# Storing query and key tiles as high and low parts already in the projection of a one-core hybrid attention block

## The chip, the cores and the metric

The kernel runs on one core of one Trainium2 chip. The time is the device time of one launch in microseconds (us). Before the change three runs took 1384.02, 1390.10 and 1389.47 us, median 1389.47. The execution that the profiler recorded took 1383.56 us.

## The reference

One decoder block on x of 1024 tokens by 1024 channels, in float32. All weights are float32 and are read once.

```
h    = modulate(rms_norm(x), sh1, sc1)              # adaLN from c
proj = h @ w_in                                     # q_d k_d v_d | iq ik iw | q_f k_f v_f | f_logit
DSA (8 heads of 64): score = sum_h iw_h relu(iq_h . ik);  keep the 256 best keys of each query
                     softmax over the kept keys, rope on the first 16 channels of q_d, k_d
FoX (8 heads of 64): softmax(q k / 8 + cum_q - cum_k), causal, cum = cumsum(log_sigmoid(f_logit + b))
x    = x + g1 * (rms_norm(o_d) | rms_norm(o_f)) @ w_out
h    = modulate(rms_norm(x), sh2, sc2);  x = x + g2 * (silu(h @ w_gate) * (h @ w_up)) @ w_down
out  = rms_norm(x)
```

## The kernel before

It is one program without loops at run time. Every engine has its list of instructions, and semaphores alone tie the lists together. Engines are named as in the profile: PE multiplies matrices, DVE (VectorE), ACT (ScalarE) and POOL (GpSimd) work on elements, SP issues all DMAs, in its own order.

A float32 product is computed as three products of fp32r operands: each operand is split into a high part (a rounding copy) and a low part (value less high). Who does the splitting, and when, is what the change is about.

**Projection.** `w_in` is taken in seven chunks (`CHUNK_COL`): chunk 0 holds what the selection and the gates need, chunks 1 to 6 hold FoX q, k, v and DSA q, k, v, in this order. A chunk of 512 columns has eight tiles of 24 matmuls (`tile`, `three`). The tiles go round four PSUM banks, so PE may start tile n once tile n-4 has been copied out (`pj_ev`). ACT copies each tile out (`evac_tile`) to one of two halves of `stage`, and SP stores it to DRAM: q and k to `qk_scratch`, laid out with channels as rows, v to `v_scratch`. POOL splits the four weight pieces of the next chunk (`split`: one CAST and one TENSOR_TENSOR of 128x1024 for each).

**Selection.** Beside the projection DVE finds for each query the 256th best score by bisection: 32 steps (`bisect`), each of four counts on DVE and two on ACT (`sign_counts`) and three to five tiny operations on 128x6 elements that form the next candidate. `PROJ_ORDER` deals the steps out over ACT's list: one or two steps between the copies of two tiles. Then `choose` turns the scores of query tiles 2 to 7 into masks, eight operations for each tile. The first `CHOICE_EARLY` operations (four tiles) come before attention, the rest are dealt out one by one over attention's units (`CHOICE_TILES`).

**Attention.** 16 heads (0 to 7 FoX, 8 to 15 DSA) of eight units, one for each query tile of 128. For unit u PE forms the logits (`logits`), DVE adds the bias and finds the minimum (`biased`), ACT takes the exponential (`expo`), PE transposes (`turn`), ACT copies out, and PE multiplies with the values of a pair of heads (`values`). Logits run two units ahead. For a head's logits PE needs the high and low parts of q and k: `load_qk` loads q and k of the head, each twice over 64 partitions, to `Qd` and `Kd`, and POOL makes the parts (`prepare`: three CASTs and two TENSOR_TENSORs, two CASTs for a DSA head). `Qd` and `Kd` exist once, so `load_qk(hd + 2)` waits until `prepare(hd + 1)` is done. The rotation of DSA's q and k (`rotate`) is done by POOL in three parts, in heads 3 to 5.

In the same stretch DVE sums the adaLN rows (`modulation`, 32 operations on 128x1024, each on a 512 KB piece of `ada_w`), at the units that `MOD_TILES` names, and POOL splits `w_out` (`split_out`) in heads 12 to 14. The last half of projection tiles 6 and 7 of chunk 6 is done in head 0 (`HELD_AT`).

**After attention** come the output projection and a feed-forward part with Strassen-like sums. The change leaves both as they are.

## Time and profile before

| | |
|---|---|
| time of the profiled execution | 1383.56 us |
| its span | 1381.8 us |
| median of three runs | 1389.47 us (1384.02 to 1390.10) |
| PE busy | 1309.9 us, 95% |
| DVE busy | 1004.5 us, 73% |
| POOL busy | 851.4 us, 62% |
| ACT busy | 695.7 us, 50% |
| granted TensorE clock, mean | 0.986 of full speed |

The profile gives for each engine the time in which it worked. Matmuls are pipelined and overlap in the listing, so a busy PE may still be slower than it could be. The share of an engine is a mean over stages that have different limits, so the stages are looked at apart: the bisection beside the projection lies at 193 to 331 us, the rest of the projection to 364 us, attention at 364 to 613 us. 1.76 us of the time lie outside the span.

### The profile page before, as it was taken

The page shows a single profiled execution, that of the slowest core. Times are in us where ns is not written, and L with a number is a line of the kernel's source. Part 1 is how long each engine was busy: PE and PEld are TensorE (multiplying, and loading weights), DVE is VectorE, ACT ScalarE, POOL GpSimd, SP SyncE. Part 2 cuts the span into 40 slices and gives each one's busy share as a digit, 9 for nine tenths or more (in the row PEclk, how much of TensorE's full clock was granted, in tenths as well). Part 3 has the DMA queues.
Part 4 walks back from the last instruction along what each step waited for, and adds up shares of the span by engine and source line. Part 5 has one row for each costly group of instructions (what it writes and reads, how often), then busy time and mean ns, then how long its engine had stood idle before and what let it go on. Part 6 is the DMA issues. An engine that isn't in the chain of part 4 may idle for free.

```text
span 1381.8 us, 19486 instructions
## 1 busy us (share of the span) xinstructions
PE 1309.9 (95%) x6595; PEld 1069.4 (77%) x6595; DVE 1004.5 (73%) x1585; ACT 695.7 (50%) x1395; POOL 851.4 (62%) x552
## 2 busy tenths in 40 slices
PE   1999999999989999999999899999999999999996
PEld 0988778888767677678887688888888888788885
DVE  4563769999786888876569776655556667479998
ACT  6623345564478777774336344333444333554545
POOL 0261403324359744951027889988889984798995
PEclk9799999999999999999999999999999999999998
DMA  9131312342345776715100333233333234998873
GB/s 382 55 98 55 97 49 92 107 124 78 100 124 168 232 218 192 215 48 198 42 36 31 105 107 123 85 115 100 115 114 109 90 122 153 390 355 300 287 255 140
DMA packets 130379, 200.53 MB, mean 145 GB/s; under 512 B 10637, under 2 KB 65093, under 8 KB 129258
## 3 DMA queue, kind: packets, MB, share of 16 engines
q1 hardware_dynamic: 130282, 199.30, 43.2%
q8 instruction: 53, 0.87, 0.3%
q14 instruction: 44, 0.36, 0.1%
HBM read 156.99 MB, written 42.27 MB: 144 GB/s over the span
## 4 chain that ended last, share of the span: by engine, by line
PE 77%; DVE 10%; issue 4%; ACT 3%; DMA 2%; POOL 2%; SPq 1%; DVEq 0%; ACTq 0%; POOLq 0%
PE PS L2176 20%; PE PS L2177 20%; PE PS L2178 20%; PE PS L2393 4%; PE PS L2345 4%; DVE AS L2042 2%; PE PS L2364 2%; DMA ada<-in_ada_w_dram 1%; DVE BS L2047 1%; POOL WSf L1025 1%; PE PS L2369 1%; PE PS L2366 1%; DVE LP L1815 1%; POOL WS L1037 1%; DVE PS L2099 1%
## 5 line engine op out<-in xcount | busy, mean ns | idle before, releaser
L1037 POOL TENSOR_TENSOR WS<-WSf,WS 128x512 fp32r<-128x512 f32 x109 | 161.7, 1491 | 9.1 <-ACT WS L1347 9.1
L1347 ACT CAST WS<-WSf 128x512 fp32r<-128x512 f32 x110 | 68.5, 623 | 195.3 <-POOL WSf L1025 194.5
L1025 POOL TENSOR_TENSOR WSf<-rawg 128x512 f32<-128x512 f32 x55 | 77.7, 1412 | 115.5 <-PE PS L2178 110.8
L2176 PE MATMUL PS<-yh,WS 128*128 128x512 f32 (+2 forms) x360 | 139.2, 387 | 1.5 <-DVE yl L1956 1.5
L2177 PE MATMUL PS<-yl,WS 128*128 128x512 f32 (+2 forms) x360 | 138.9, 386 | 0.0
L2178 PE MATMUL PS<-yh,WS 128*128 128x512 f32 (+2 forms) x360 | 138.8, 385 | 0.0
L2176 PE MATMUL PS<-BS,AS 128*128 128x512 f32 x308 | 121.0, 393 | 3.9 <-DVE BS L2047 3.1
L2177 PE MATMUL PS<-BS,AS 128*128 128x512 f32 x308 | 120.4, 391 | 0.0
L2178 PE MATMUL PS<-BS,AS 128*128 128x512 f32 x308 | 120.3, 391 | 0.0
L1268 ACT ACTIVATE LP<-LP,nmin 128x128 f32<-128x128 f32 (+7 forms) x128 | 100.2, 783 | 36.5 <-DVE nmin L1815 35.1
L2042 DVE TENSOR_TENSOR AS<-rawa,AS 128x512 fp32r<-128x512 f32 x77 | 100.1, 1316 | 23.5 <-ACT AS L1406 23.3
L2176 PE MATMUL PS<-XH,WS 128*128 128x512 f32 x264 | 103.6, 392 | 6.2 <-POOL WS L1037 6.2
L1056 POOL TENSOR_TENSOR BS<-rawb,BS 128x512 fp32r<-128x512 f32 x57 | 90.4, 1591 | 27.9 <-ACT BS L1410 27.7
L2178 PE MATMUL PS<-XH,WS 128*128 128x512 f32 x264 | 103.3, 391 | 0.0
L2177 PE MATMUL PS<-XL,WS 128*128 128x512 f32 x264 | 103.2, 391 | 0.0
L1657 DVE TENSOR_SCALAR_CACHE_REDUCE marks_c<-sel,bis 128x640 f32<-128x640 f32 (+4 forms) x134 | 102.5, 819 | 0.6
L2345 PE MATMUL PS<-ident,LP 128*128 128x128 f32 x576 | 89.1, 279 | 8.1 <-ACT PTb L1258 3.7
L1049 POOL TENSOR_TENSOR rawb<-rawb 128x512 f32<-128x512 f32 x55 | 90.1, 1648 | 7.5 <-DMA rawb<-in_w_down_dram 7.5
L1170 ACT ACTIVATE PS<-sel,bis 128x896 f32<-128x896 f32 x64 | 67.6, 1057 | 49.9 <-DVE bis L1712 35.1
L2345 PEld LDWEIGHTS PS<-ident,LP 128*128 128x128 f32 x576 | 64.9, 141 | 30.5 <-ACT PTb L1258 9.7
L1025 POOL TENSOR_TENSOR WSf<-rawu 128x512 f32<-128x512 f32 x55 | 84.6, 1538 | 3.0 <-PE PS L2178 2.5
L1406 ACT CAST AS<-rawa 128x512 fp32r<-128x512 f32 x77 | 47.9, 622 | 76.0 <-PE PS L2178 64.8
(340 smaller groups left out, 3836.0 us busy)
## 6 DMA issues: line engine op xcount, KB each, us to landing
rawb<-in_w_down_dram SPq DMA_DIRECT2D x132, 256.0 KB, 4.8
rawa<-gu_scratch SPq DMA_DIRECT2D x77, 256.0 KB, 4.8
gu_scratch<-GS SPq DMA_DIRECT2D x55, 256.0 KB, 4.8
raw<-in_w_in_dram SPq DMA_DIRECT2D x24, 512.0 KB, 3.9
rawg<-in_w_gate_dram SPq DMA_DIRECT2D x22, 512.0 KB, 4.5
rawu<-in_w_up_dram SPq DMA_DIRECT2D x22, 512.0 KB, 4.4
ada<-in_ada_w_dram SPq DMA_DIRECT2D x8, 1024.0 KB, 15.1
qk_scratch<-stage SPq DMA_DIRECT2D x32, 256.0 KB, 2.2
```

The lines of the kernel that those rows point to most:

```text
L1025: pool.tensor_tensor(WSf[m % N_SLOT][:], left(i, mat, a), left(i, mat, b), ALU.add if sign > 0 else ALU.subtract).then_inc(ws_sum, 1)
L1037: pool.tensor_tensor(lo, WSf[m % N_SLOT][:] if b else left(i, mat, a), hi.bitcast(F32), ALU.subtract).then_inc(ws_ready, 1)
L1049: pool.tensor_tensor(r[:, 0, :], r[:, 0, :], r[:, 1, :], ALU.add if RIGHT[DOWN[m // PAIRS]][2] > 0 else ALU.subtract).then_inc(gb_sum, 1)
L1056: pool.tensor_tensor(b[:, 1, :], rawb[m % DOWN_RAW_B][:, 0, :], b[:, 0, :].bitcast(F32), ALU.subtract).then_inc(gb_lo, 1)
L1268: act.activation(LP[:, u % 3, 0:n], LP[:, u % 3, 0:n], ACT.Exp, bias=nmin[:, u:u + 1], scale=-1.0, accum_out=sums[:, u:u + 1]).then_inc(ex ...
L1347: act.copy(WS[m % N_SLOT][:, 0], src).then_inc(ws_hi, 1)
L1657: did(dve.tensor_scalar(marks[0][:, n_tk % 2, 0:P * (t + 1)], view(t), limit, 0.0, op, ALU.add, accum_out=col(0, t)))
L2042: dve.tensor_tensor(AS[m % DOWN_SLOTS][:, 1, :], rawa[m % DOWN_RAW_A][:], AS[m % DOWN_SLOTS][:, 0, :].bitcast(F32), ALU.subtract).then_inc ...
L2176: pe.matmul(dst, left[0], right[0], start=first, stop=False)
L2177: pe.matmul(dst, left[0], right[1], start=False, stop=False)
L2178: return pe.matmul(dst, left[1], right[0], start=False, stop=last)
L2345: last = pe.transpose(dst[:, i * P:(i + 1) * P], src, ident[:])
```

## The change

- The chunks are taken in the order 0, FoX v, FoX q, FoX k, DSA q, DSA k, DSA v. `TURNED`, the chunks of q and k, becomes 2, 3, 4, 5 in place of 1, 2, 4, 5.
- For a tile of q or k ACT copies out twice, once to `stage` as float32 and once to `stage_h` as fp32r, the high part. POOL subtracts the two to `stage_l` (`low_tile`). SP waits for the subtraction and stores high and low part, two DMAs of 256 KB for one before.
- `load_qk` loads the parts from DRAM to where PE reads them, six DMAs of 256 KB for four before, and waits until PE has read the logits of head hd - 2 (`qk_pe`). `Qd`, `Kd` and `prepare` are gone. Head 1 gets a place of its own.
- The rotation adds high and low, rotates and splits again, twelve operations of 128x1024 in one run on POOL for six in three runs. Its loads and stores double.
- Three query tiles are chosen before attention for four before, and 24 operations of `choose` for 16 lie inside it, in heads 0 to 4.
- No modulation lies in head 4, and four lie in head 5.
- `split_out` is no longer tied to heads: POOL does it when the data is there.

```diff
-CHUNK_COL = [COL_IDX, COL_FOX, COL_FOX + GW, COL_FOX + 2 * GW, 0, GW, 2 * GW]
+CHUNK_COL = [COL_IDX, COL_FOX + 2 * GW, COL_FOX, COL_FOX + GW, 0, GW, 2 * GW]
-CHOICE_TILES = ((2, 4, 6, 7), (1, 2, 3, 5, 6, 7), (1, 2, 3, 5, 6, 7))
+CHOICE_TILES = ((2, 4, 6, 7), (1, 3, 5, 6, 7), (1, 2, 3, 5, 6, 7), (1, 3, 5, 6, 7), (1, 2, 3, 4))
-MOD_TILES = {hd: (6, 7) if hd < 6 else (1, 2, 6, 7) for hd in (*range(4, 12), 13)}
+MOD_TILES = {hd: (1, 2, 6, 7) for hd in (*range(5, 12), 13)}
-CHOICE_EARLY = 4 * CHOICE_OPS
+CHOICE_EARLY = 3 * CHOICE_OPS
-TURNED = (1, 2, 4, 5)
-VALUES = (3, 6)
+TURNED = (2, 3, 4, 5)
+VALUES = (1, 6)
+LOW_AHEAD = ((0, 1), (2,), (3,), (4,))
...
             def load_qk(hd):
                 b, first, row = hd % 2, 0 if hd < NH else 2, hd % NH * DH
-                if hd >= 1:
-                    sp.wait_ge(k_lo, hd)
-                    sp.wait_ge(q_lo, hd)
-                for i, dst in enumerate((Qd, Kd)):
-                    for half in range(2):
-                        sp.dma_start(dst[half * DH:(half + 1) * DH, :],
-                                     qk_dram[first + i, row:row + DH, :]).then_inc(qk_in[b], 16)
+                i = qk_home(hd)
+                if hd >= 2:
+                    sp.wait_ge(qk_pe, TT * (hd - 1))
+                q_high, q_low, k_high, k_low = (dram[first + e, row:row + DH, :] for e in range(2) for dram in (qk_dram, qk_low_dram))
+                sp.dma_start(QT[i][0:DH, :].bitcast(F32), q_high).then_inc(qk_in[b], 16)
+                sp.dma_start(KA[i][0:DH, :].bitcast(F32), k_high).then_inc(qk_in[b], 16)
+                sp.dma_start(QT[i][DH:P, :].bitcast(F32), q_low).then_inc(qk_in[b], 16)
+                sp.dma_start(KA[i][DH:P, :].bitcast(F32), k_high).then_inc(qk_in[b], 16)
+                if hd < NH:
+                    sp.dma_start(CQ[0:DH, b, :].bitcast(F32), q_high).then_inc(qk_in[b], 16)
+                    sp.dma_start(CK[0:DH, b, :].bitcast(F32), k_low).then_inc(qk_in[b], 16)
...
                     sp.wait_ge(pj_ev, TT * ch + t + 1)
                     if ch in TURNED:
+                        sp.wait_ge(pj_lo, TT * (ch - TURNED[0]) + t + 1)
...
-                if hd == 1:
+                if hd == 3:
                     sp.wait_ge(qk_pe, TT)
+                    sp.wait_ge(tp_ev, group_no["C", 3] + 1)
                     for i in range(2):
-                        sp.dma_start(RX[i][:], rope_rows(i)).then_inc(rx_in, 16)
+                        sp.dma_start(RX[i][:], rope_rows(qk_dram, i)).then_inc(rx_in, 16)
+                        sp.dma_start(RT[i][:], rope_rows(qk_low_dram, i)).then_inc(rx_in, 16)
...
-                if hd >= 1:
-                    load_qk(hd + 2)
+                load_qk(hd + 2)
...
+            def low_tile(ch, t):
+                n = TT * (ch - 1) + t
+                pool.wait_ge(pj_ev, TT * ch + t + 1)
+                pool.tensor_tensor(stage_l[:, n % 2, :], stage[:, n % 2, :], stage_h[:, n % 2, :].bitcast(F32),
+                                   ALU.subtract).then_inc(pj_lo, 1)
...
-            def prepare(hd):
-                b, i = hd % 2, 0 if hd == 0 else 2 - hd % 2
-                pool.wait_ge(qk_in[b], 64 * (hd // 2 + 1))
-                if hd >= 2:
-                    pool.wait_ge(qk_pe, TT * (hd - 1))
...
                 if n >= 2:
-                    act.wait_ge(stage_out[n % 2], 16 * (n // 2))
-                act.mul(stage[:, n % 2, :], PS[:, q % 4, :], -SOFT if ch in (1, 4) else 1.0).then_inc(pj_ev, 1)
+                    act.wait_ge(stage_out[n % 2], stores_ahead(n))
+                last = act.mul(stage[:, n % 2, :], PS[:, q % 4, :], QK_SCALE.get(ch, 1.0))
+                if ch in TURNED:
+                    last = act.mul(stage_h[:, n % 2, :], PS[:, q % 4, :], QK_SCALE[ch])
+                last.then_inc(pj_ev, 1)
...
                 if t == 0:
-                    pe.wait_ge(k_lo, hd + 1)
-                    pe.wait_ge(q_lo, hd + 1)
+                    pe.wait_ge(qk_in[hd % 2], 96 * (hd // 2 + 1))
```

The first place is POOL's list in the projection, where the weight pieces of the next chunk are split. `wl`, `wh` are weights, `raw` the loaded piece. Before:

```order
L898 CAST wl<-raw 128x1024
L900 TENSOR_TENSOR wl<-raw,wl 128x1024
L898 CAST wl<-raw 128x1024
L900 TENSOR_TENSOR wl<-raw,wl 128x1024
L898 CAST wh<-raw 128x1024
L900 TENSOR_TENSOR wh<-raw,wh 128x1024
```

Now, at the same splits:

```order
L924 CAST wl<-raw 128x1024
L926 TENSOR_TENSOR wl<-raw,wl 128x1024
L932 TENSOR_TENSOR stagel<-stage,stageh 128x512
L924 CAST wl<-raw 128x1024
L926 TENSOR_TENSOR wl<-raw,wl 128x1024
L932 TENSOR_TENSOR stagel<-stage,stageh 128x512 x5
L924 CAST wh<-raw 128x1024
L926 TENSOR_TENSOR wh<-raw,wh 128x1024
```

Every tile of a q or k chunk brings one subtraction (L932) between the splits. Three of the five in a row belong to the end of one chunk, two to the start of the next.

The second place is SP's list at the first pieces of `ada_w` for the modulations (`adar`), with what the DMA waits for. Before, in the pass for head 3:

```order
L672 DMA Qd<-qk_scratch 64x1024 [waits q_lo,k_lo]
L672 DMA Qd<-qk_scratch 64x1024
L672 DMA Kd<-qk_scratch 64x1024 x2
L663 DMA Vn<-v_scratch 128x4x128 [waits pv_pe]
L663 DMA Vn<-v_scratch 128x4x128
L776 DMA g1b<-in_ada_b_dram 1x1024 [waits md_ms]
L776 DMA mod<-in_ada_b_dram 1x1024 x2
L725 DMA adar<-in_ada_w_dram 128x1024 [waits tk_done]
```

Now, in the pass for head 4:

```order
L685 DMA QT<-qk_scratch 64x1024 [waits qk_pe]
L686 DMA KA<-qk_scratch 64x1024
L687 DMA QT<-qk_low_scratch 64x1024
L688 DMA KA<-qk_scratch 64x1024
L690 DMA CQ<-qk_scratch 64x1024
L691 DMA CK<-qk_low_scratch 64x1024
L749 DMA adar<-in_ada_w_dram 128x1024 [waits tk_done]
L749 DMA adar<-in_ada_w_dram 128x1024
```

The first modulation stood at unit 6 of head 4 and stands at unit 1 of head 5. Its piece now comes behind the six loads of head 6, and these wait until PE has done the last logits of head 4.

## Rows read from the trace of the kernel before

**Rows 1.** DVE in time, around the bisection: start us, us, line, operation

```profile
193.41 0.17 DVE L1692 TENSOR_TENSOR bis<-bis 128x6 f32<-128x6 f32 x1
...
207.21 2.29 DVE L1692 TENSOR_TENSOR bis<-bis 128x6 f32<-128x6 f32 x1
...
233.86 0.61 DVE L1657 TENSOR_SCALAR_CACHE_REDUCE marks_c<-sel,bis 128x384 f32<-128x384 f32 x1
...
236.92 0.17 DVE L1692 TENSOR_TENSOR bis<-bis 128x6 f32<-128x6 f32 x1
...
237.32 0.17 DVE L1712 TENSOR_TENSOR bis<-bis 128x6 f32<-128x6 f32 x1
...
237.52 0.61 DVE L1657 TENSOR_SCALAR_CACHE_REDUCE marks_c<-sel,bis 128x384 f32<-128x384 f32 x1
...
330.23 0.17 DVE L1692 TENSOR_TENSOR bis<-bis 128x6 f32<-128x6 f32 x1
```

**Rows 2.** POOL in time, one weight split of the projection

```profile
207.09 2.39 POOL L900 TENSOR_TENSOR wh<-raw,wh 128x1024 fp32r<-128x1024 f32 x1
```

**Rows 3.** POOL's 128x512 subtraction elsewhere: ns shortest/median/longest, first and last start

```profile
L1037 POOL TENSOR_TENSOR WS<-WSf,WS x109: 1263/1304/2246, 717.7 to 1140.2; 128x512 fp32r<-128x512 f32 x109
```

**Rows 4.** ACT in time, copies of projection tiles: [idle before <-releaser]

```profile
236.04 0.58 ACT L1145 ACTIVATE stage<-PS 128x512 f32<-128x512 f32 x1
...
328.81 1.06 ACT L1145 ACTIVATE stage<-PS 128x512 f32<-128x512 f32 x2
...
336.69 0.60 ACT L1145 ACTIVATE stage<-PS 128x512 f32<-128x512 f32 x1 [4.56 <-PE PS L2178]
```

**Rows 5.** DVE in time, the last tile chosen before attention and the first bias

```profile
353.78 0.61 DVE L1741 TENSOR_SCALAR sel<-sel,bis 128x768 f32<-128x768 f32 x1
...
360.10 0.56 DVE L1764 TENSOR_SCALAR sel<-sel 128x768 f32<-128x768 f32 x1
364.21 0.29 DVE L1815 CUSTOM_DVE_ANT_0 LP<-PS,strip 128x128 f32<-128x128 f32 x1 [3.55 <-PE PS L2366]
```

**Rows 6.** Stretches, attention by pairs of heads: us, busy by engine, clock, DMA share, GB/s

```profile
193.00:331.00 138.00, 138.00 (x610) 114.28 (x609) 131.47 (x370) 82.43 (x149) 46.32 (x29) 1.00 0.32 101
...
364.00:393.30 29.30, 26.15 (x161) 20.20 (x160) 24.56 (x45) 21.70 (x54) 21.46 (x12) 1.00 0.52 140
393.30:425.90 32.60, 29.92 (x221) 22.47 (x222) 23.11 (x44) 24.75 (x63) 21.30 (x12) 1.00 0.30 71
...
456.20:485.00 28.80, 26.54 (x191) 19.47 (x189) 25.23 (x45) 23.00 (x59) 20.78 (x10) 1.00 0.79 255
485.00:514.70 29.70, 29.52 (x224) 22.95 (x224) 23.49 (x42) 23.05 (x61) 15.09 (x9) 1.00 0.72 231
514.70:545.50 30.80, 28.75 (x213) 21.20 (x209) 26.70 (x48) 24.43 (x61) 16.08 (x9) 1.00 0.63 189
545.50:582.00 36.50, 34.59 (x241) 25.88 (x243) 29.09 (x58) 28.00 (x67) 26.98 (x14) 0.95 0.68 202
582.00:613.00 31.00, 29.39 (x204) 20.88 (x205) 28.84 (x61) 24.56 (x62) 19.95 (x11) 1.00 0.34 103
```

**Rows 7.** SP, POOL and PE in time, from the load of head 8 to its logits

```profile
470.06 1.12 SPq L672 DMA_DIRECT2D Qd<-qk_scratch  x2
...
477.15 1.04 POOL L935 CAST QT<-Qd 128x1024 fp32r<-128x1024 f32 x1 [7.17 <-DMA Kd<-qk_scratch]
...
481.73 3.23 POOL L943 TENSOR_TENSOR QT<-Qd,QT 64x1024 fp32r<-64x1024 f32 x1
...
485.04 1.09 SPq L672 DMA_DIRECT2D Qd<-qk_scratch  x2
...
485.07 0.30 PE L2364 MATMUL PS<-KA,QT 128*128 128x128 f32 x1 [0.88 <-issue]
```

**Rows 8.** DVE's modulations of one kind: ns shortest/median/longest

```profile
L1830 DVE SCALAR_TENSOR_TENSOR mod<-adax,cact,mod x14: 1274/1280/3368, 473.2 to 580.8; 128x1024 f32<-128x1024 f32 x14
```

**Rows 9.** DVE in time, a choice and a modulation beside busy POOL

```profile
405.58 3.36 DVE L1756 SCALAR_TENSOR_TENSOR marks_d<-marks_d,bis 128x1024 f32<-128x1024 f32 x1
...
580.82 3.37 DVE L1830 SCALAR_TENSOR_TENSOR mod<-adax,cact,mod 128x1024 f32<-128x1024 f32 x1
```

More of the change, by code:

```diff
@@ L203, with stores_through, stores_ahead @@
     GB_TARGET.append((GB_TARGET[_m - DOWN_RAW_B] if _m >= DOWN_RAW_B else GB_BASE[_m]) + (32 if _m in DOWN_SUMS else 16))
-GU_BASE = dict(zip(DOWN, 2 * [8 * (NC - 1) * TT] + [16 * MOD_SLOT.count(0), 16 * MOD_SLOT.count(1)] + 2 * [64 * V_PARTS] + [16]))
+GU_BASE = dict(zip(DOWN, 2 * [8 * TT * (NC - 1 + len(TURNED))] + [16 * MOD_SLOT.count(0), 16 * MOD_SLOT.count(1)] + 2 * [64 * V_PARTS] + [16]))
+def stores_through(ch):
+    return 8 * TT * sum(2 if c in TURNED else 1 for c in range(1, ch + 1))
+def stores_ahead(n):
+    return sum(32 if 1 + m // TT in TURNED else 16 for m in range(n % 2, n, 2))
 def done_first(t):
@@ L355, in build @@
         g1b = at(32, "g1b", [P, D])
-        QT = [at(kb, f"QT{i}", [P, SEQ], F32R) for i, kb in enumerate((180, 40, 52))]
-        KA = [at(kb, f"KA{i}", [P, SEQ], F32R) for i, kb in enumerate((184, 44, 56))]
+        QT = [at(kb, f"QT{i}", [P, SEQ], F32R) for i, kb in enumerate((180, 40, 52, 172))]
+        KA = [at(kb, f"KA{i}", [P, SEQ], F32R) for i, kb in enumerate((184, 44, 56, 176))]
         KB = [at(kb, f"KB{i}", [P, SEQ], F32R) for i, kb in enumerate((188, 48, 60))]
@@ L686, in _ @@
             for ch in range(1, NC):
-                if ch == 5:
-                    for i in range(2):
-                        sp.wait_ge(stage_out[i], 16 * 3 * TT // 2)
-                    sp.wait_ge(sc_pe, IH * (TT - FIRST_TOPK))
-                    load_qk(0)
                 if ch == 6:
@@ L696, in _ @@
                     load_cum(1)
+                    for i in range(2):
+                        sp.wait_ge(stage_out[i], stores_through(3))
+                    sp.wait_ge(sc_pe, IH * (TT - FIRST_TOPK))
+                    load_qk(0)
                 for t in range(TT):
@@ L700, in _ @@
                     if ch in TURNED:
+                        sp.wait_ge(pj_lo, TT * (ch - TURNED[0]) + t + 1)
+                    if ch in TURNED:
                         f, half = divmod(t, 2)
-                        dst = qk_dram[QK_BASE[ch], f * P:(f + 1) * P, half * BANK:(half + 1) * BANK]
-                    else:
-                        dst = v_dram[VALUES.index(ch), t * P:(t + 1) * P, :]
-                    sp.dma_start(dst, stage[:, q % 2, :]).then_inc(stage_out[q % 2], 16)
+                        for dram, held in ((qk_dram, stage_h), (qk_low_dram, stage_l)):
+                            sp.dma_start(dram[QK_BASE[ch], f * P:(f + 1) * P, half * BANK:(half + 1) * BANK],
+                                         held[:, q % 2, :].bitcast(F32)).then_inc(stage_out[q % 2], 16)
+                    else:
+                        sp.dma_start(v_dram[VALUES.index(ch), t * P:(t + 1) * P, :], stage[:, q % 2, :]
+                                     ).then_inc(stage_out[q % 2], 16)
                     if t < PIECES and ch + 1 < NC:
                         load_piece(PIECES * (ch + 1) + t)
-                    if ch == 6 and t == 4:
+                    if ch == 6 and t == 2:
+                        for i in range(2):
+                            sp.wait_ge(stage_out[i], stores_through(5))
                         load_qk(1)
-                    if ch == 6 and t == TT - 2:
-                        load_qk(2)
                 if ch == 4:
@@ L904, in _ @@
                 w = IDXW if ch == 0 else GW
+                if ch - 1 in TURNED:
+                    for t in LOW_AHEAD[n % PIECES]:
+                        low_tile(ch - 1, t)
                 if ch == 0:
@@ L916, in _ @@
                 split(n, hi[:, 0:2 * w], lo[:, 0:2 * w], held, rounded=ch == 0).then_inc(w_ready, 1)
+                if ch - 1 in TURNED and n % PIECES == PIECES - 1:
+                    for t in range(LOW_AHEAD[-1][-1] + 1, TT):
+                        low_tile(ch - 1, t)
             pool.wait_ge(pj_pe, (NC - 1) * TT)
             pool.wait_ge(w_ready, N_PROJ)
+            pool.wait_ge(pj_lo, TT * len(TURNED))
             pool.memset(CQ[DH:DH + 4].bitcast(F32), 1.0).then_inc(strip_ok, 1)
@@ L986, in _ @@
                 pool.tensor_copy(spread[i][:], angle[:].unsqueeze(2).to_broadcast([P, TT, REPS, HALF])).then_inc(spread_ok, 1)
-            for hd in range(2 * NH):
-                if 1 <= hd and hd + 1 < 2 * NH:
-                    prepare(hd + 1)
-                    if hd + 1 in ROPE_HEADS:
-                        rotate(ROPE_HEADS.index(hd + 1))
-                    if hd == 3:
-                        for dst in (g1b, mod23):
-                            pool.memset(dst[:], 0.0).then_inc(md_ms, 1)
-                    if hd == 9:
-                        pool.wait_ge(tp_ev, group_no["M", 5] + 1)
-                        pool.memset(mod23[:, 0, :], 0.0).then_inc(md_ms, 1)
-                for k in WO_ORDER:
-                    if WO_HEAD.get(k) == hd:
-                        split_out(k)
-            for k in WO_ORDER[-len(wo_late):]:
+            pool.wait_ge(tp_ev, group_no["C", 3] + 1)
+            for dst in (g1b, mod23):
+                pool.memset(dst[:], 0.0).then_inc(md_ms, 1)
+            rotate()
+            pool.wait_ge(tp_ev, group_no["M", 5] + 1)
+            pool.memset(mod23[:, 0, :], 0.0).then_inc(md_ms, 1)
+            for k in WO_ORDER:
                 split_out(k)
```

95 lines of the change are left out of this document (45 added, 50 removed).

## The prediction, made before the changed kernel was run

> **What bounds the kernel now.** I read the table of stretches first, since the change touches only the projection and attention (193 to 613 us of the span); then each engine in order of time around the bisection, at the seam at 364 us, and at the turn from one head to the next.
>
> In the stretch with the bisection PE is busy all of its 138 us and DVE 131.5 [rows 6]. PE sets the end there, but DVE is close behind and ACT hangs on both: ACT's list alternates counts, which need DVE's candidate, with the copies that free PE's banks. A step of the bisection takes 3.66 us when nothing disturbs it (233.86 to 237.52). Its counts take the first 3.06 us, its tiny operations on 128x6 start at 3.06, 3.26, 3.46 and 3.54 [rows 1]. From the first step to the last the tiny operation L1692 starts 32 times, at 193.41 and last at 330.23 [rows 1]: 136.8 us for 31 steps against 31 x 3.66 = 113.5. The reader is to see where the missing 23 us lie: at 207.21 L1692 takes 2.29 us for 0.17, and POOL's subtraction runs from 207.09 to 209.48 [rows 1, 2]. A tiny operation that starts beside a running POOL operation ends with it. The counts keep their 0.61 us. Twelve weight splits lie in the stretch; less some 3 us in which the first two steps waited for ACT, they cost 20 us, 1.7 each.
>
> In attention no one engine is full. The fastest pair of heads takes 28.8 us, the others up to 36.5 [rows 6]. In 485 to 514.7 us PE is busy 29.5 of 29.7 us, so about 28.8 to 29.5 is what PE asks for in a full pair, and only the excess of the other pairs can be won. Two things make it. One is the same block as above: a modulation takes 1.27 us alone and 3.37 at 580.82, an operation of the choice 3.36 at 405.58 [rows 8, 9]. The other is a loop of SP and POOL: the load for head 8 is issued at 470.06, has landed at 477.15, POOL has made the parts at 484.96, and only then the next load is issued, at 485.04 [rows 7]. 15.0 us a head, as long as a head lasts, and at 485.07 PE begins head 8 right behind it, after 0.88 us of idleness.
>
> **The change part by part.**
>
> *The second copy on ACT.* 32 copies, 0.48 us each behind the first (two in a row take 1.06 [rows 4]). In a step ACT counts 2.2 us and copies, 236.04 being 2.18 into the step: with two copies it is done at 3.24, inside the 3.66 of the step. Cost nothing by itself; if DVE's steps did not cover it, it would be at most 0.48 x 32 = 15 us on an engine with 82 of 138 us busy.
>
> *The subtraction on POOL.* 32 of 128x512, at least 1.26 us each [rows 3]. It starts when ACT's second copy is done, so at 3.3 into a step, when DVE is behind and ACT copies at once. Then it runs to 4.56 and catches DVE's third tiny operation, due at 3.46: 1.1 us. Of the 24 tiles copied during the bisection (tiles 6 and 7 of chunk 2 to tile 5 of chunk 5) the first four come while ACT still waits for PE: 20 x 1.1 = 22 us. A weight split that comes right behind a subtraction blocks two operations of the same step and no third, so I take 1.1 for 1.7, 12 x 0.6 = 7 less. The idle 3 us of the first steps take up as much again, which leaves DVE about 12 us later at the last step. Ends: if the subtractions met the steps at random, 1.26 x (1.26 / 2 + 0.6) / 3.66 = 0.42 us each, 10 less 7 is 3; if each cost its whole length, 24 x 1.26 = 30, less 3 for the early wait is 27. I take 12, since the start of the subtraction is tied to the step by ACT's list.
>
> The Trainium skill has the rule behind this (SBUF — State Buffer, on what contends inside SBUF): the engines share one port pair, held for a whole instruction by the one that starts first, and the other blocks fully. The trace agrees (2.29 us for 0.17 [rows 1]). By the rule alone the sum would be the same with 1.1 us for a subtraction, since it starts first and is held to its end.
>
> *What it does to PE.* Tile 2 of chunk 6 needs tile 6 of chunk 5 copied out. That copy ended at 329.4 (328.81 plus half of 1.06), the tile began at 336.69, when its forerunner was complete [rows 4]: 7.3 us to spare. So 12 us more on the steps stop PE for about 5 to 6. I take 6. On DVE's side the choice of tile 5 leaves the path, 353.78 to 360.66, 6.9 us, and 3.55 us were idle before the first bias [rows 5]: 12 - 6.9 - 3.5 = 2, less than 6. So attention starts 6 us later; ends 0 and, with 27 us on DVE, 27 - 7.3 = 20. In chunk 2 six more subtractions fall beside the scores, where DVE was waiting for others part of the time: 1, ends 0 and 2.
>
> *Preparation gone from attention.* POOL loses 15 preparations, and the loop with them. The load for head hd + 2 now needs only the logits of head hd, and has a head's length, 14 to 15 us, to land: six loads by the 7.1 us that four took [rows 7] make 10.6. Over 28.8 us the pairs of rows 6 stand at 3.8 (393.3), 0.9 (485), 2.0 (514.7), 7.7 (545.5) and 2.2 (582). The splits of w_out stay in the last two, so does the choice in the second. I take back 1.5, 0.5, 1.5, 4.5 and 1.0, and 1.5 in the first pair, where two blocked operations of the choice and one preparation lie: 10.5 us. Ends: 1 (only the idleness before head 8) and 17, the whole excess. The pair at 426 wins nothing, POOL's rotation fills it.
>
> *The rotation in one run.* Ten TENSOR_TENSORs at 2.4 and two copies at 1.04 are 26 us, over 30 with DVE in the way, from the second half of head 3 into head 5. Nine operations of the choice now lie in heads 3 and 4 beside it, and tile 5 adds eight operations, 6.9 us of DVE, to attention. With PE's lookahead of two units I count a fifth of 6.9 and 9 x 0.1: 2 us, ends 0 and 5.
>
> *The first modulation.* Its 512 KB come behind the six loads of head 6, which wait for the last logits of head 4. From there: issue of six, 3.6 us by the 1.1 for two, landing of 2 MB by four loads' 7.1 some 9.5. DVE reaches unit 1 of head 5 after two short biases, about 2 us. 7.5 us of waiting, and every bias of the head is queued behind it, then ACT and PE. PE has two units in hand: 5 us. Ends 0 (if PE's queue of values covers it) and 9.
>
> *More DMA.* Half a megabyte more for each head beside 189 to 255 GB/s now [rows 6]; the pieces for units 6 and 7 are issued behind the loads and land about when they are due: 1 us, ends 0 and 5.
>
> Sum: 6 + 1 - 10.5 + 2 + 5 + 1 = +4.5 us on 1383.56, so 1388 for an execution like the profiled one. Two of three runs lie 6 us above it and one beside it; the mean of all four is 1387, and I give 1391 as the median to come.
>
> **The rivals.**
>
> *The window is missed: faster.* If the subtraction starts late enough (a step is only open from 1.8 to 3.6 us), or the tiny operations slip in between, DVE loses 3 us and the 7.3 hide it. With DVE less pressed at the seam too, I count 0 for the bisection, 0.5 for the scores, -12 for the preparation, 1 for the rotation, 2 for the modulation, 0.5 for the DMA: -8, so 1387 - 8 = 1379. For it: the median modulation beside POOL takes 1.28 us, as long as the shortest [rows 8], so overlap does not always mean a block. Against it: the start is tied to the step.
>
> *The bisection becomes the bound: slower.* Every subtraction costs its length, the steps reach 4.9 us where PE's tiles pay for 4.1 (three tiles of 5.44 for four steps). Then PE stands at bank waits from chunk 5 on: 27 - 7.3 = 20 in place of 6, 4.5 + 14 = +18: 1405. It decides from 7.3 us of added delay on. For it: the lag of ACT's copies is there today. Against it: tiny operations that come before 3.3 get through.
>
> *Loads late: slower.* If six loads and two pieces need over 14 us beside each other, each of 13 heads waits 1 to 2 us: +13 in place of +1, +16: 1403. Against it: 10.6 us by the row.
>
> **How the numbers follow.** The forecast 0.44, the missed window 0.27, the bisection as the bound 0.22, late loads 0.07. What a measurement of this kernel can tell from no change is about 0.5%, 7 us. Of the missed window 0.22 lie past it, and 0.05 within. The forecast's own range is 1382 to 1399, -5 to +12; of its 0.44 I put 0.04 below -7, 0.32 within and 0.08 above +7. With the two slower cases this gives faster 0.26, same 0.37, slower 0.37. The range for 8 in 10 goes from 1376, in the missed window's lower part, to 1404, beside the centre of the two slower cases; some 0.06 is left out below and 0.13 above.
>
> **What would show it.** Right: L1692 in the changed profile often over 1 us in chunks 3 to 5, 32 starts over some 149 us; PE idle a few us before 364 + 6 with a wait for ACT's copy; the first bias at about 371; a hole on DVE at unit 1 of head 5 that ends with the landing of adar; pairs of heads at 29 to 30 us and 32 where 36.5 stood. Wrong: 32 starts in 140 us or in over 160; no hole at head 5; logits at a head's start waiting for a load; pairs no shorter than now, which would mean that neither the loop nor the block made them.

## The result, and the profile after

The changed kernel took 1402.11 us (median of 5 runs, 1396.17 to 1403.44), the kernel before 1387.66 (5 runs, 1384.02 to 1390.10). The ratio is 1.0092, 95% interval 1.0066 to 1.0118: slower by about 13 us. The forecast was 1391, 1376 to 1404, so the range held the time and its centre was 11 us too low. The profiled execution after took 1403.44 us, 19.9 more than the one before; the two medians lie 14.4 apart, so some 5 us of what follows are those two executions' own scatter.

The page of the changed kernel, engines and granted clock:

```profile
PE 1316.5 (94%) x6595; PEld 1074.3 (77%) x6595; DVE 983.0 (70%) x1585; ACT 711.0 (51%) x1427; POOL 773.1 (55%) x518
...
PEclk8899999999998999999999999999999999999998
...
HBM read 166.43 MB, written 51.71 MB: 156 GB/s over the span
```

DVE has 21 us less to do and POOL 78 less, and still the kernel is slower; the mean clock fell from 0.986 to 0.979. Where it happened is read best head by head. The first bias of a head (128x128) comes at these times of the span:

| head | 0 | 3 | 4 | 5 | 6 | 8 | 12 | 15 |
|---|---|---|---|---|---|---|---|---|
| before | 364.21 | 412.82 | 425.93 | 441.95 | 456.84 | 485.97 | 546.39 | 600.42 |
| after | 369.43 | 415.74 | 432.88 | 456.30 | 477.53 | 508.63 | 566.38 | 620.03 |
| later by | 5.2 | 2.9 | 7.0 | 14.4 | 20.7 | 22.7 | 20.0 | 19.6 |

So all of it is there when head 6 begins. Heads 8 to 11 win 2.7 us, and what follows attention is the same within 0.3. The stretches of the changed kernel, columns as in [rows 6]: head 0, heads 3, 4 and 5, then heads 6 and 7, 8 and 9, 10 and 11.

```profile
369.43:384.47 15.04, 14.07 (x69) 11.33 (x68) 9.04 (x23) 8.43 (x23) 2.03 (x2) 0.90 0.14 52
...
415.74:432.88 17.14, 12.47 (x89) 9.71 (x88) 9.73 (x24) 11.55 (x29) 0.09 (x1) 0.93 1.04 225
432.88:456.30 23.42, 20.31 (x123) 14.26 (x122) 17.52 (x23) 12.46 (x31) 23.12 (x9) 0.83 0.38 86
456.30:477.53 21.23, 14.96 (x92) 11.29 (x91) 11.36 (x22) 11.42 (x29) 6.43 (x4) 0.84 0.82 227
477.53:508.63 31.10, 30.03 (x220) 22.20 (x220) 23.09 (x46) 23.53 (x61) 0.00 (x0) 1.00 1.02 315
508.63:537.80 29.17, 28.53 (x218) 21.98 (x213) 22.98 (x45) 23.79 (x63) 0.95 (x1) 1.00 0.96 279
537.80:566.38 28.58, 28.11 (x210) 21.07 (x208) 23.00 (x45) 23.46 (x61) 0.00 (x0) 1.00 0.85 243
```

Four places have a wait of their own. The first is the end of the projection, ACT's copies of tiles 0 to 5 of chunk 6 and SP beside them (it answers to [rows 4, 5]):

```profile
343.35 0.60 ACT L1160 ACTIVATE stage<-PS 128x512 f32<-128x512 f32 x1 [0.65 <-DMA qk_low_scratch<-stagel]
357.20 1.21 ACT L1160 ACTIVATE stage<-PS 128x512 f32<-128x512 f32 x2 [13.25 <-DMA v_scratch<-stage]
...
368.07 0.60 ACT L1160 ACTIVATE stage<-PS 128x512 f32<-128x512 f32 x1 [6.03 <-DMA v_scratch<-stage]
```

```profile
346.83 0.49 SPq L685 DMA_DIRECT2D QT<-qk_scratch  x1
...
351.30 6.85 SPq L728 DMA_DIRECT2D v_scratch<-stage  x3
358.25 0.45 SPq L685 DMA_DIRECT2D QT<-qk_scratch  x1
...
361.94 7.07 SPq L728 DMA_DIRECT2D v_scratch<-stage  x3
```

Tiles 0 and 1 were copied at 342.1 and 343.35, but SP stood at its wait for POOL's strips (constant rows that POOL writes behind its last subtraction) and then issued six loads, so the first store of a value tile left at 351.30. By the trace's semaphore events, which all landing times here are taken from, it landed at 357.12, behind the last of the six loads (356.51). `stage` has two halves: the copy of tile 2 waited 13.25 us for it. PE stopped twice in this stretch, first for ACT's second copy of a key tile and then for the copy that came late by the stores:

```profile
337.95 0.50 PE L2194 MATMUL PS<-wh,hh 128*128 128x512 f32 x1 [1.40 <-ACT stageh L1162]
...
368.81 0.30 PE L2380 MATMUL PS<-KA,QT 128*128 128x128 f32 x1 [3.35 <-ACT stage L1160]
```

The second and third place are the start of head 4 and what follows in it, on SP, POOL, PE and DVE in turn:

```profile
412.90 0.45 SPq L685 DMA_DIRECT2D QT<-qk_scratch  x1
...
416.65 0.57 SPq L777 DMA_DIRECT2D RX<-qk_scratch  x1
...
419.19 0.45 SPq L703 DMA_DIRECT2D CK<-cum_scratch  x1
```

The last of head 4's six loads, issued at 415.95, in the view of DMA issues of 412 to 419.1 (KB, us from issue to landing):

```profile
CK<-qk_low_scratch SPq DMA_DIRECT2D x1, 256.0 KB, 6.5
```

```profile
432.79 4.67 POOL L973 TENSOR_TENSOR RX<-RX,RT 128x1024 f32<-128x1024 f32 x2 [19.85 <-DMA RT<-qk_low_scratch]
```

```profile
432.05 0.45 PE L2380 MATMUL PS<-KA,QT 128*128 128x128 f32 x1 [4.56 <-issue]
```

```profile
432.88 0.29 DVE L1833 CUSTOM_DVE_ANT_0 LP<-PS,strip 128x128 f32<-128x128 f32 x1 [5.44 <-PE PS L2382]
...
435.17 4.44 DVE L1770 TENSOR_TENSOR_SCAN marks_d<-marks_d 128x1024 f32<-128x1024 f32 x1
...
439.99 2.88 DVE L1774 SCALAR_TENSOR_TENSOR marks_d<-marks_d,bis 128x1024 f32<-128x1024 f32 x1
...
443.40 2.78 DVE L1778 SCALAR_TENSOR_TENSOR sel<-sel,bis,marks_d 128x1024 f32<-128x1024 f32 x1
```

Head 4's six loads (1.5 MB) are issued from 412.90 on and have all landed at 422.49. Behind them stand 2 MB for the rotation, and behind those the two 8 KB loads of the cumulative sums (`cum_scratch`) of head 4, issued at 419.19 and 419.68. Head 4's logits wait for these two as well (`ckb_in` in the kernel). They landed at 431.96 and PE began at 432.05; the profile names no releaser there. The last of the 2 MB landed at 432.72 and POOL began at 432.79. 2 MB in the 10.2 us from 422.49 are 205 GB/s by my estimate; the stretch from 415.74 shows 225 GB/s and a DMA share of 1.04. Then POOL rotates, and the last tile of the choice lies beside it on DVE. The fourth place is the one foreseen, unit 1 of head 5:

```profile
464.42 1.28 DVE L1848 SCALAR_TENSOR_TENSOR g1b<-adar,cact,g1b 128x1024 f32<-128x1024 f32 x1 [6.66 <-DMA adar<-in_ada_w_dram]
```

Behind each of these stops PE's clock is lower, which no term of the prediction had. Short stretches around the first of them in head 4:

```profile
424.00:427.40 3.40, 3.40 (x27) 2.13 (x25) 3.40 (x8) 2.86 (x9) 0.00 (x0) 1.00 1.04 235
427.40:432.00 4.60, 0.09 (x2) 0.00 (x0) 0.04 (x1) 1.22 (x3) 0.00 (x0) 0.84 1.02 230
432.00:434.50 2.50, 2.45 (x11) 2.33 (x11) 0.30 (x2) 0.83 (x2) 1.71 (x1) 0.50 1.04 220
434.50:437.50 3.00, 3.00 (x15) 1.79 (x15) 2.68 (x3) 1.10 (x4) 2.96 (x2) 0.53 1.02 215
437.50:441.00 3.50, 3.50 (x26) 2.32 (x25) 3.50 (x4) 2.52 (x8) 3.46 (x1) 1.00 0.73 169
```

PE works 0.09 of 4.6 us and then goes at 0.50, the 1.2 GHz level, for over 5 us. The price is seen in one product with the values, 128x256:

```profile
435.06 0.63 PE L2409 MATMUL PS<-PTa,Vn 128*64 128x256 f32 x1
...
438.74 0.38 PE L2409 MATMUL PS<-PTa,Vn 128*64 128x256 f32 x1
```

Over heads 0, 3, 4 and 5 the missing clock is 0.10 x 15.0 + 0.07 x 17.1 + 0.17 x 23.4 + 0.16 x 21.2 = 10 us; before, the clock was 1.00 in all four. That is an upper bound of its price, since PE was not the bound in all of it.

### The profile page after: what moved, and what is told of

Same layout as the page of the kernel before. It is cut to its first block, busy times and chain, and to the rows that moved or that the text cites. A ratio compares the mean times of both kernels' runs of the same rounds, so it can differ in the third digit from the quotient of the medians.

```text
span 1401.7 us, 19543 instructions
## 1 busy us (share of the span) xinstructions
PE 1316.5 (94%) x6595; PEld 1074.3 (77%) x6595; DVE 983.0 (70%) x1585; ACT 711.0 (51%) x1427; POOL 773.1 (55%) x518
## 4 chain that ended last, share of the span: by engine, by line
PE 66%; DVE 15%; issue 6%; DMA 4%; ACT 4%; POOL 2%; SPq 2%; DVEq 0%; ACTq 0%; POOLq 0%
PE PS L2194 17%; PE PS L2195 16%; PE PS L2196 16%; DVE marks_c L1675 5%; PE PS L2409 4%; PE PS L2363 4%; DVE AS L2060 2%; PE PS L2380 2%; DMA ada<-in_ada_w_dram 2%; DVE BS L2065 1%; POOL WSf L1040 1%; PE PS L2382 1%; PE PS L2385 1%; DMA v_scratch<-stage 1%; DVE bis L1710 1%
## 5 line engine op out<-in xcount | busy, mean ns | idle before, releaser
L932 POOL TENSOR_TENSOR stagel<-stage,stageh 128x512 fp32r<-128x512 f32 x32 | 41.3, 1292 | 127.9 <-ACT stageh L1162 127.8
L2380 PE MATMUL PS<-KA,QT 128*128 128x512 f32 (+1 forms) x192 | 77.7, 404 | 18.5 <-DVE nmin L1833 10.4
```

Of the source, the lines that this page charges most:

```text
L2380: pe.matmul(dst, q, KA[i][:, b:b + w], start=True, stop=False)
```

## The experiments

Each was timed beside the kernel before; 0.1% is 1.4 us. "Start" is counted from the bisection's first step, since that lies at 190.1 to 193.4 in the executions: it is 170.8 us to the first bias before and 176.2 after.

**One edit of order at a time.** First, in chunk 6, the store of value tile 0 ahead of the strips and head 0's loads (the block moves into the loop over tiles, and head 1's loads from tile 2 to tile 4):

```diff
-                if ch == 6:
-                    sp.wait_ge(strip_ok, 4)
...
+                    if ch == 6 and t == 0:
+                        sp.wait_ge(strip_ok, 4)
...
-                    if ch == 6 and t == 2:
+                    if ch == 6 and t == 4:
```

> In chunk 6 SP now issues the store of value tile 0 before it waits for POOL's four strip operations and loads q and k of head 0; the loads of head 1 move behind the store of tile 4. Nothing else is changed. Theory A (the order of SP's list costs the time at the seam): ACT's copy of tile 2 no longer waits 13.25 us for a store, the first bias comes at 364 to 366 in place of 369.43, the second 1.7 us after it in place of 3.1, and the whole is 4 to 7 us faster than the changed kernel, 1396 to 1398, ratio to the kernel before about 1.005. Rival B (PE is late because the bisection is longer, the store only ends last): PE stops as long as now, at bank waits in chunks 5 and 6, the first bias stays at 368 to 370, the ratio at 1.008 to 1.010. Rival C (whatever attention gains at its start is given back at head 4, whose loads are timed by others): first bias earlier by 5, head 6 earlier by less than 2.

1397.16 us, ratio 1.0078 (1.0061 to 1.0095). The start took 172.5, head 0 13.5 us for 15.0, and the gain stayed: 5.2 us at the bias of head 15. That falls under theory A in the trace: PE's stop of 3.35 us is gone. By the ratios the gain is 2 us, not told apart from none. ACT's wait had only moved by a tile: the copy of tile 3 waited 11.76 us, for the store of tile 1 that still stood behind the six loads. PE did not wait for it.

```profile
357.22 1.21 ACT L1160 ACTIVATE stage<-PS 128x512 f32<-128x512 f32 x2 [11.76 <-DMA v_scratch<-stage]
```

Second, the high parts for the rotation:

```diff
-                if hd == 3:
+                if hd == 2:
                     sp.wait_ge(qk_pe, TT)
-                    sp.wait_ge(tp_ev, group_no["C", 3] + 1)
                     for i in range(2):
                         sp.dma_start(RX[i][:], rope_rows(qk_dram, i)).then_inc(rx_in, 16)
+                if hd == 3:
+                    sp.wait_ge(tp_ev, group_no["C", 3] + 1)
+                    for i in range(2):
                         sp.dma_start(RT[i][:], rope_rows(qk_low_dram, i)).then_inc(rx_in, 16)
```

> The two loads of the high parts for the rotation (RX, 1 MB) are issued in SP's iteration 2, right behind the loads of head 3, where now they follow the loads of head 4; the two of the low parts (RT, 1 MB) stay. Theory A (3.5 MB share the DMA engines at some 225 GB/s, so head 4's 1.5 MB land at 432): with 1 MB less between, they land 4 to 4.5 us sooner, the bias of head 4 waits under 1.5 us for PE in place of 5.44, PE does not drop to its lower clock at 432, and the whole is 4 to 7 us faster than the changed kernel, ratio about 1.005. Rival B (the loads of head 4 are late since they are issued only at 412.9, and DMAs are served in their order): landing and wait stay within 1 us of now, ratio 1.008 to 1.010. Rival C (head 4 is set by the choice beside POOL's rotation, 13.7 us of DVE in one piece from 435 to 449, which starts with the loads too): head 4 begins 4 us earlier and head 5 at most 1 us earlier.

1398.66 us, ratio 1.0092 (1.0074 to 1.0109). In the trace the effect is theory A's, the reason is not: the bias of head 4 waits 0.59 us, and head 3 lasts 12.3 us for 17.1, but head 4's six loads landed at 422.40, within 0.1 us of the changed kernel, as rival B says. What came earlier is the cumulative sums, 426.70 for 431.96, since 1 MB less stands in front of them; the logits began at 427.27. Head 4 shrinks by 1.4 as well, and the bias of head 15 comes 6 us sooner. The times do not show it: against the changed kernel's 1.0092, with both intervals near 0.2%, a gain up to 3 or 4 us is not excluded, 6 hardly fits. What took the rest in the timed runs is open.

```profile
427.88 0.29 DVE L1835 CUSTOM_DVE_ANT_0 LP<-PS,strip 128x128 f32<-128x128 f32 x1 [0.59 <-PE PS L2384]
```

Third, the first modulation's pieces:

```diff
+                if hd == 4:
+                    load_mod(0)
+                    load_mod(1)
+                    n_mod = 2
                 load_qk(hd + 2)
```

> The pieces for modulations 0 and 1 are issued before the six loads of head 6, not behind them, as soon as the last choice has freed their place. Theory A (the modulation at unit 1 of head 5 waits for its piece, and biases, ACT and PE are queued behind it): the wait of 6.66 us at 464.42 goes, under 1 us is left, and the granted clock of 449 to 481 rises from 0.93 and 0.80 towards 1; 5 to 8 us faster than the changed kernel, ratio about 1.004 to 1.006. Rival B (PE's two units of lookahead and a late landing of head 6's loads take its place): the wait goes, but logits of head 6 wait for their loads as long, the whole gains under 2 us, ratio 1.008 to 1.010.

1395.99 us, ratio 1.0075 (1.0051 to 1.0099). SP issues the two at 448.69, the wait is gone, heads 4 and 5 together take 39.6 us for 44.7: 5.0 us, at the lower end of theory A; at the bias of head 15 2.7 us are left, and by the ratios 2.4. The modulations now meet the end of the rotation instead, 1.96 and 3.19 us for 1.28.

```profile
455.93 1.96 DVE L1852 SCALAR_TENSOR_TENSOR g1b<-adar,cact,g1b 128x1024 f32<-128x1024 f32 x1
...
459.12 3.19 DVE L1852 SCALAR_TENSOR_TENSOR g1b<-adar,cact,g1b 128x1024 f32<-128x1024 f32 x1
```

**The three together** (the edits as above).

> The three edits of the order of SP's list together: store first in chunk 6, high parts for the rotation loaded one iteration earlier, first modulation's pieces ahead of head 6's loads. Theory A (three separate stops whose prices add up, the lower clock behind each included): 13 to 20 us faster than the changed kernel, 1382 to 1390, ratio to the kernel before 0.995 to 1.002. Rival B (one of them hides the others, or a common limit such as DMA volume or the longer bisection lies behind all): the gain is that of the best single one, 5 to 7 us, ratio about 1.005. If the change had brought the 10.5 us that the prediction took back in attention, this kernel would reach 0.992 or less.

1388.27 us (12 runs), ratio 1.0010 (0.9992 to 1.0029). From 1.0092 that is 11 us, more than any single one gave and just under theory A's 13. In the traces the prices add up: the bias of head 15 comes 5.2, 6.0 and 2.7 us sooner in the single edits and 13.8 here. By the ratios the three single gains come to 4 us only; with intervals of about 0.2% on each that is not settled.

**Head 0's loads later still**, behind tile 2, head 1's behind tile 5.

```diff
-                    if ch == 6 and t == 0:
+                    if ch == 6 and t == 2:
...
-                    if ch == 6 and t == 4:
+                    if ch == 6 and t == 5:
```

> As the first experiment, with head 0's loads behind the store of value tile 2 of chunk 6 and head 1's behind that of tile 5: all stores that a copy waits for are issued, and have landed, before 1.5 MB of loads come. Theory A (in the first experiment the store of tile 1 was still issued behind six loads, at 351.4, and landed beside them at 357): the copy at 357.22 with its 11.76 us wait comes at 348 to 350, no copy waits over 3 us for a store, the first bias comes at 362 to 365, 1 to 3 us before that of the first experiment, ratio about 1.006. Rival B (PE's own work ends at 364 whatever the stores do): first bias at 365 to 366, as there, ratio 1.0078 again. Rival C (head 0's loads now land too late): logits of head 0 wait for them, first bias after 367.

1397.12 us, ratio 1.0063 (1.0039 to 1.0087). From tile 3 on the copies now wait for PE alone, one in 5.44 us, and the start takes 171.5 us, 1.0 less than in the first experiment and 0.7 more than before the change. But that 1.0 is PE's wait for the second copy of a key tile, 0.36 us here and 1.29 there, which this edit does not touch. Four later executions with the same edit have starts of 172.1 to 172.5, against 172.5 and 172.6 with the first edit. So nothing shows that the later loads gained: rival B.

```profile
346.78 0.60 ACT L1160 ACTIVATE stage<-PS 128x512 f32<-128x512 f32 x1 [3.74 <-PE PS L2196]
352.22 0.60 ACT L1160 ACTIVATE stage<-PS 128x512 f32<-128x512 f32 x1 [4.84 <-PE PS L2196]
```

**The subtraction cut short**, on the kernel above.

```diff
-                pool.tensor_tensor(stage_l[:, n % 2, :], stage[:, n % 2, :], stage_h[:, n % 2, :].bitcast(F32),
+                pool.tensor_tensor(stage_l[:, n % 2, 0:16], stage[:, n % 2, 0:16], stage_h[:, n % 2, 0:16].bitcast(F32),
```

> The kernel e5_loads_after_tile2 with POOL's subtraction cut to 16 of its 512 columns, the rest of the low part left at zero: stores, waits and counts are the same, so only the length of the 32 subtractions is taken away. The prediction's theory (each subtraction blocks a tiny operation of the bisection for 1.1 us, and PE stops for about 6 us at the end of chunk 5 because of it): 32 starts of the tiny operation over 134 to 138 us in place of 144.5, first bias 4 to 7 us earlier than in e5_loads_after_tile2. My theory now (the bisection is longer by 7.7 us, but PE's 7.3 us of slack take it; what was late at the seam were stores and loads): starts over 134 to 138 us, first bias at most 1.5 us earlier, the whole within 2 us of e5_loads_after_tile2.

1394.32 us (12 runs), ratio 1.0048 (1.0032 to 1.0065). The 32 starts take 130.4 us, which is less than either theory gave. The starts of the tiny operation, the first group of this kernel, the second of the one that it is compared with:

```profile
L1714 DVE TENSOR_TENSOR bis<-bis x32: 165/166/2160, 190.1 to 320.5; 128x6 f32<-128x6 f32 x32
```

```profile
L1710 DVE TENSOR_TENSOR bis<-bis x32: 165/166/1693, 191.9 to 335.3; 128x6 f32<-128x6 f32 x32
```

So the subtractions cost DVE 13 us net: the weight splits hold more when the subtractions are short (see the account below). The start is 170.85 for 171.5: of those 13 us PE feels 0.7. In the kernel above PE is busy 143.30 of the 143.40 us of the bisection; its slack took the rest, as my theory then said.

**The choice packed into heads 0 to 3**, on the changed kernel.

```diff
-CHOICE_TILES = ((2, 4, 6, 7), (1, 3, 5, 6, 7), (1, 2, 3, 5, 6, 7), (1, 3, 5, 6, 7), (1, 2, 3, 4))
+CHOICE_TILES = ((1, 2, 3, 4, 5, 6, 7), (1, 2, 3, 4, 5, 6, 7), (1, 2, 3, 4, 5, 6, 7), (1, 2, 3))
```

> The changed kernel with its 24 late operations of the choice packed into heads 0 to 2 and the first units of head 3, so that none lies beside POOL's rotation in head 4. Theory A (head 4 takes 23.4 us since three operations of the choice are blocked there and DVE is busy in one piece from 435 to 449): heads 0 to 2 stay within 1 us of their lengths, since DVE is busy only 9 to 12 of 16 us there, head 4 takes 16 to 18 us, and the whole is 4 to 6 us faster than the changed kernel, ratio about 1.005. Rival B (head 4's length comes from PE's lower clock after the stop at 427 and from the late loads): head 4 stays over 21 us, the ratio at 1.008 to 1.010. Rival C (the choice only moves its cost into heads 0 to 2): heads 0 to 2 together longer by 3 us or more, no net gain.

1402.47 us, ratio 1.0105 (1.0080 to 1.0130): no gain by the times. Head 4 fell to 18.2 us for 23.4, as A says, but head 0 rose to 17.7 for 15.0, near what C says; by the trace 2.5 us were left at head 15. The crowding of head 0, beside its held tiles, was not foreseen.

**All four together**, with the later loads.

> All edits of order together: stores first, head 0's and head 1's loads behind tiles 2 and 5, high parts for the rotation loaded an iteration earlier, first modulation's pieces before head 6's loads, the choice packed into heads 0 to 3. Theory A (prices add up: 11 us for the three of before, 1 to 2 for the later loads, 5 for the choice): ratio to the kernel before 0.995 to 0.998, the bias of head 6 at 454 to 458 where the kernel before has it at 456.84. Rival B (the choice is hidden once the stop before head 4 is gone): ratio 1.000 to 1.001, head 6 at 460 to 462. Rival C (attention really was to gain 10.5 us from the lost preparation, and these stops only hid it): ratio 0.990 or less, heads 6 to 15 shorter than the kernel before by 5 us or more.

1385.54 us (12 runs), ratio 0.9987 (0.9969 to 1.0006): not told apart from the kernel before, and 1.05%, nearly 15 us, under the changed one. By the trace that is theory A, with the bias of head 6 at 455.07; by the ratio it stands just above A's 0.998. Rival C is out. Head 4 lasts 15.8 us with the same rotation beside it and a full clock. Heads 3, 4 and 5 of this kernel:

```profile
413.05:425.52 12.47, 11.95 (x84) 8.79 (x83) 9.59 (x22) 10.64 (x28) 1.53 (x1) 1.00 0.94 208
425.52:441.31 15.79, 15.79 (x122) 11.71 (x121) 6.84 (x18) 12.21 (x31) 15.55 (x8) 1.00 0.76 198
441.31:455.07 13.76, 12.71 (x93) 9.76 (x92) 12.09 (x22) 11.22 (x29) 10.27 (x5) 1.00 0.99 267
```

Since the trace of this kernel is of an execution that took 1377.79 us, 8 under its median, I compare only lengths of heads with it.

**The preparation put back**, without its loop, for heads 7 to 12, on the kernel with all four.

```diff
+            for hd in range(7, 13):
...
+                pool.wait_ge(qk_in[hd % 2], 96 * (hd // 2 + 1))
+                pool.tensor_copy(QT[3][:], RL[0][:].bitcast(F32)).then_inc(extra, 1)
+                pool.tensor_copy(KA[3][:], RL[1][:].bitcast(F32)).then_inc(extra, 1)
...
+                pool.tensor_tensor(QT[3][:], RL[0][:].bitcast(F32), RL[1][:].bitcast(F32), ALU.subtract).then_inc(extra, 1)
```

> The kernel e8_all_four, with POOL doing in heads 7 to 12 what it did before the change: as soon as a head's loads have landed two copies and two subtractions on 128x1024 (half the partitions in the last), on dead tiles, so that nobody waits for them. Only the block of DVE's modulations and the port come back, not the loop of SP and POOL. The prediction's theory (the block and the loop made the excess of the pairs, 10.5 us in all): heads 7 to 13 together 4 to 8 us longer than in e8_all_four, ratio to the kernel before 1.003 to 1.005. My theory now (in those heads DVE is busy 11.6 of 15 us and PE all but full, so DVE has room for the blocks, and nothing was won by their going): heads 7 to 13 within 2 us of e8_all_four, ratio 0.998 to 1.001.

1390.81 us (12 runs), ratio 1.0026 (1.0005 to 1.0046), 0.39% above 0.9987. In the trace heads 7 to 13 are longer by 1.5 us and head 6, in which the first preparation falls, by 2.0. The prediction's 4 to 8 us in those heads are not there, my 2 us held by the heads. The ratio lies between the two, above my 1.001. Head 7 lasts 15.8 to 18.5 us in the kernels of this group that have no such block, so 3.5 us is a rough figure. Heads 8 and 9, this kernel and then the one with all four (before the change they took 31.40 us):

```profile
491.29:522.73 31.44, 29.74 (x219) 22.50 (x220) 28.98 (x45) 23.84 (x61) 18.49 (x10) 1.00 0.92 262
```

```profile
486.39:515.57 29.18, 28.55 (x218) 21.99 (x214) 22.99 (x46) 23.81 (x63) 0.95 (x1) 1.00 0.97 279
```

DVE's busy time rises by 6 us for the same work, the pair by 2.3: about a third of what DVE loses arrives at the end of this pair.

**Two of six loads cut** from head 11 on, on the kernel with all four.

```diff
+                w = SEQ if hd < NH + 3 else 16
+                sp.dma_start(KA[i][DH:P, 0:w].bitcast(F32), k_high[:, 0:w]).then_inc(qk_in[b], 16)
...
+                    sp.dma_start(KB[i][DH:P, 0:w].bitcast(F32), k_low[:, 0:w]).then_inc(qk_in[b], 16)
```

> The kernel e8_all_four, with two of the six loads of each head from head 11 on (the second copies of k's high and low part) cut to 16 of 1024 columns: the computation of those heads is left with stale values there; the moved data falls from 1.5 to 1 MB a head, what it was before the change. Theory A (the DMA engines, at a share of 0.8 to 1.05 of their time there, hold the heads up and have eaten the gain): heads 11 to 15 together 3 us or more shorter than in e8_all_four. Theory B (loads have landed before they are asked for, PE sets the pace): the same lengths within 1 us, the whole within 2 us.

1386.71 us (12 runs), ratio 0.9999 (0.9981 to 1.0018). Heads 11 and 12 last 13.0 and 17.4 us in both; heads 13 and 14 took 1.4 us more, not less. Theory B for those heads. It says nothing of heads 6 and 7, where the transfers are densest.

**The choice spread otherwise**, on the kernel with all four.

```diff
+CHOICE_TILES = ((2, 4, 6, 7), (1, 2, 3, 4, 5, 6, 7), (1, 2, 3, 4, 5, 6, 7), (1, 2, 3, 5, 6, 7))
```

> The kernel e8_all_four with another place for the choice: head 0 keeps its four operations, heads 1 and 2 take seven, head 3 six, head 4 none. In e8_all_four head 0 lasts 16.35 us for 13.5 in e5_loads_after_tile2, since seven operations lie beside its held tiles. Theory A (the only price is that crowding of head 0): head 0 at 13.5 to 14, head 3 at most 1 us longer, head 6 begins 1.5 to 2.5 us sooner, ratio to the kernel before 0.997 to 0.998. Rival B (the operations cost DVE the same wherever they stand before the rotation): what head 0 gives, head 3 takes, ratio 0.998 to 1.000.

1385.61 us (12 runs), ratio 0.9990 (0.9972 to 1.0008). Head 0 gave 2.8 us, head 3 took 2.7: rival B. Head 7 lasted 18.5 us here, 15.8 with all four and 17.4 in the experiment before; that scatter I did not settle.

## Why the prediction was right and wrong

Step by step, in the executions shown (+19.9 us):

- **Projection and bisection, +6: measured +5.2, the size right by luck, the path to it wrong.** The mechanism on DVE is there. A step with a subtraction on the changed kernel, first DVE, then POOL:

```profile
236.72 1.17 DVE L1730 TENSOR_TENSOR bis<-bis 128x6 f32<-128x6 f32 x1
...
240.99 0.17 DVE L1710 TENSOR_TENSOR bis<-bis 128x6 f32<-128x6 f32 x1
```

```profile
236.58 1.29 POOL L932 TENSOR_TENSOR stagel<-stage,stageh 128x512 fp32r<-128x512 f32 x1 [3.98 <-ACT stageh L1162]
```

  It starts where it was expected and holds the third tiny operation; from 236.32 the step takes 4.66 us, against 3.66 undisturbed [rows 1]. In the whole bisection 21 of 25 subtractions hold a tiny operation, by 20.5 us in all, against the 20 x 1.1 = 22 of the forecast. Mis-sized was what the weight splits give back: before, they held tiny operations by 21.4 us, on the changed kernel by 7.8 (11.9 with the subtractions cut short). So the whole grew by 7.7 us, 144.5 for 136.8, where I had 12. PE's 7.3 us of slack took nearly all of it, and PE stopped for 1.40 us and not for 5 to 6. Most of the rest, 3.35 us, came from a row of SP's list that I had not read: POOL's strips now wait for the last subtraction, head 0's loads stand behind them, and value stores behind both.
- **Preparation gone, -10.5: about -7.** Without the stops heads 0 to 3 take 57.1 us for 61.7 (the three together), heads 8 to 11 57.8 for 60.4, the rest nothing. That the lost preparation is the reason is not shown for heads 0 to 3, where the choice and the rotation moved too. Putting the block back cost 3.5 us by the trace in heads 6 to 14. The split over the pairs was off: 4.5 was taken at the pair from 545.5 to 582. Its heads 12 and 13 last 37.5 us for 37.7, with PE busy 35.5 and 35.7, so the excess was mostly how PE's work falls over the pairs. Reading an excess over the fastest pair as winnable was the error.
- **The rotation in one run, +2: measured about +12, the step that failed.** Its ten operations on POOL were priced, its four loads were only counted. They take 2 MB in SP's queue, in front of two 8 KB loads that head 4's logits wait for, and that held head 3 to 17.1 us for 12.3. Logits waiting for a load is one of the prediction's own signs of being wrong. And the choice beside the rotation was priced at a fifth of its blocks. Without PE's stop before it head 4 still lasts 22.0 to 22.5 us (the second experiment and the three together), against 15.8 once the operations stand elsewhere.
- **First modulation, +5: right.** 6.66 us of waiting for 7.5, head 5 longer by 6.3, and 5.0 us come back in heads 4 and 5 when the piece is issued earlier. The piece landed 10.9 us after the first of the six loads was issued. The 9.5 us for 2 MB do not follow from the row of the prediction: scaled as for the six loads, the four loads' 7.1 us give 14.2. So the nearness is in part luck.
- **More DMA, +1: about +2**, in heads 6 and 7 (31.1 us for 29.1), with the DMA share at 1.02. That the transfers do it is likely: modulations wait 1.53 us (at 505.08) and 0.9 us for their pieces there, and none waited in these heads before. No run here took the transfers away.
- **The clock** was in no term.

None of the rivals happened. "Loads late" came closest in time, 1403, by accident: head 4's six loads took 9.6 us from the first issue to the last landing, for the 10.6 of the forecast. What was late was another, far smaller load, once and by 4.6 us. "The bisection becomes the bound", 1405, is out: PE stood 1.40 us and not 20. So is the missed window, since the subtractions do hold the tiny operations. The sum with the measured sizes: 5.2 + 1.5 (head 0, behind the late stores) - 4.6 (heads 0 to 3) + 4.8 (the loads in front of head 4) + 7.4 (head 4) + 6.3 (head 5) + 2.0 (heads 6 and 7) - 2.7 (heads 8 to 11) - 0.1 = 19.8.

The idea itself was neutral here: with the order mended the kernel stands where it stood, 0.9987, though POOL has 78 us less to do. Most likely that is because neither POOL nor DVE was the bound; putting a part of the work back cost 0.39%, so a little was won.

## What to carry to other kernels

When a change adds a wait or a transfer to an in-order DMA list, go down the list from there and write beside every later row who waits for it; three rows in the wrong order cost 11 us here. Look at the small rows too: a load of 8 KB, issued behind 2 MB that nobody awaits yet, comes when they have come. And read in the kernel every semaphore that a stopped engine waits for, where the profile names no releaser. Do not take the longest and shortest of unequal pieces of work as waste to be won.
